# First attention: selected and local scores of two head groups as two 64-row tiles, job pairs on one output bank

## What is computed

```python
ks = partial_rope(rms_norm(k_s, ks_gain), cos_t, sin_t)
k_blocks = ks.reshape(B, n_sel, SEL_LEN, G, Dh)      # n_sel = 512 / 64 = 8, top = min(8, 8)
s = jnp.einsum('bqgrd,bgqnld->bgrqnl', qi, kg).astype(f32) * scale
s = jnp.where(mask, s, NEG)                          # keys at or before the query
p = softmax(s); o_s = einsum(p, vg)
# local branch: the same with kw, vw, over the last WINDOW = 256 positions and the query itself
# MLA: 8 heads, 96 query/key dimensions, 64 value dimensions, causal
```

## Time and profile before

| | us |
|---|---|
| median of 3 runs | 2212.72 |
| lowest, highest | 2210.98, 2212.72 |
| span of the profiled execution | 2210.5 |
| TensorE busy in it | 2158.2 (98%) |
| VectorE, ScalarE, GpSimd busy | 1498.9, 946.0, 1195.8 |
| first attention, first NSA score to first MLA score | 209.4 to 300.8 |

### The profile page before, as it was taken

The page is one execution under the profiler, slowest core; times in us unless marked ns, Lnnn a source line. Parts: engine busy times, 40 slices in busy tenths (PEclk is TensorE's granted clock), DMA queues, the critical chain, the costliest instruction groups (busy, mean ns, idle before and its releaser), DMA issues.

```text
span 2210.5 us, 33160 instructions
## 1 busy us (share of the span) xinstructions
PE 2158.2 (98%) x12377; PEld 1842.0 (83%) x12377; DVE 1498.9 (68%) x2234; ACT 946.0 (43%) x1891; POOL 1195.8 (54%) x594
## 2 busy tenths in 40 slices
PE   6999999999999999999999999999999999999997
PEld 4788888877899988887887898888897887889886
DVE  6834777554666592897646777677996727777676
ACT  3254663011556510544743555512545725455412
POOL 4747403776477677745016654577653037544675
PEclk9999999999999999999999999999999999999999
DMA  8322102522133233222002222322322002222221
GB/s 323 153 77 89 55 30 84 190 89 96 58 115 107 105 140 133 93 105 86 1 1 95 96 78 113 113 95 79 113 81 75 1 32 84 86 106 115 95 95 57
DMA packets 32776, 206.78 MB, mean 94 GB/s; under 512 B 4080, under 2 KB 4336, under 8 KB 11632
## 3 DMA queue, kind: packets, MB, share of 16 engines
q1 hardware_dynamic: 32192, 200.27, 24.8%
q10 hardware_dynamic: 432, 4.46, 0.5%
HBM read 202.61 MB, written 2.10 MB: 93 GB/s over the span
## 4 chain that ended last, share of the span: by engine, by line
PE 88%; DVE 6%; issue 1%; ACT 1%; DMA 1%; DVEq 1%; POOL 1%; POOLq 0%; SPq 0%; ACTq 0%
PE PS L1126 18%; PE PS L1128 18%; PE PS L1127 18%; PE PS L1605 5%; PE PS L1617 5%; PE PS L1382 3%; PE PS L1381 3%; PE PS L1383 3%; PE PS L1631 3%; PE PS L1457 2%; PE PS L1459 2%; PE PS L1458 2%; PE PS L1256 1%; PE PS L1259 1%; PE PS L1258 1%
## 5 line engine op out<-in xcount | busy, mean ns | idle before, releaser
L665 POOL TENSOR_TENSOR w_hi<-raw,zero_c 128x512 fp32r<-128x512 f32 (+1 forms) x135 | 281.6, 2104 | 545.5 <-PE PS L1128 544.3
L669 POOL TENSOR_TENSOR w_lo<-raw,w_hi 128x512 fp32r<-128x512 f32 (+1 forms) x135 | 365.0, 2723 | 5.8
L1126 PE MATMUL PS<-b_hi,w_hi 128*128 128x512 f32 x512 | 203.1, 397 | 0.9 <-POOL w_lo L888 0.9
L1127 PE MATMUL PS<-b_lo,w_hi 128*128 128x512 f32 x512 | 203.0, 396 | 0.0
L1128 PE MATMUL PS<-b_hi,w_lo 128*128 128x512 f32 x512 | 203.0, 396 | 0.0
L3345 DVE TENSOR_TENSOR b_lo<-a_all,b_hi 128x512 fp32r<-128x512 f32 x44 | 162.6, 3733 | 49.3 <-ACT b_hi L2490 49.3
L1126 PE MATMUL PS<-f_hi,w_hi 128*128 128x512 f32 x448 | 177.6, 397 | 0.7 <-DVE f_lo L2647 0.7
L1128 PE MATMUL PS<-f_hi,w_lo 128*128 128x512 f32 x448 | 177.6, 396 | 0.0
L1127 PE MATMUL PS<-f_lo,w_hi 128*128 128x512 f32 x448 | 177.6, 396 | 0.0
L688 POOL TENSOR_TENSOR w_lo<-raw,w_hi 128x512 fp32r<-128x512 f32 x48 | 70.9, 1477 | 92.9 <-ACT w_hi L2482 92.9
L1126 PEld LDWEIGHTS PS<-b_hi,w_hi 128*128 128x128 f32 x512 | 96.4, 188 | 24.6 <-POOL w_lo L888 1.1
(11 more groups left out here) (586 smaller groups left out, 6868.7 us busy)
## 6 DMA issues: line engine op xcount, KB each, us to landing
raw<-slabs_dram SPq DMA_DIRECT2D x161, 1024.0 KB, 4.8
aux<-ada_dram SPq DMA_DIRECT2D x18, 512.0 KB, 5.7
ada_first<-ada_dram SPq DMA_DIRECT2D x11, 512.0 KB, 14.1
cmpw<-cmpw_dram ACTq DMA_DIRECT2D x2, 2048.0 KB, 12.7
ada_late<-ada_dram SPq DMA_DIRECT2D x8, 512.0 KB, 3.2
ada_last<-ada_dram SPq DMA_DIRECT2D x8, 512.0 KB, 6.4
xT<-xT_dram SPq DMA_DIRECT2D x1, 2048.0 KB, 9.3
out_dram<-t SPq DMA_DIRECT2D x4, 512.0 KB, 3.2
```

Source lines behind the costliest of these rows:

```text
L665: high = nc.gpsimd.tensor_tensor(w_hi[:, slot, c], raw[:, slot, c], zero[:, 0:c.stop - c.start], ALU.add)
L669: low = nc.gpsimd.tensor_tensor(w_lo[:, slot, c], raw[:, slot, c], w_hi[:, slot, c].bitcast(f32), ALU.subtract)
L1126: nc.tensor.matmul(out, a_hi_, b_hi_, start=start, stop=False)
L1127: nc.tensor.matmul(out, a_hi_, b_lo_, start=False, stop=False)
```

## The change

The jobs of one head index r and one branch b come as twins: group 0's job directly ahead of group 1's, with equal masks and key ranges. Their query and key slices are cut to the 64 partitions of their group. `Plan` weaves a twin's tiles: (m, j=3), (m+1, j=3), (m, 0), (m+1, 0), (m, 2), (m+1, 2), (m, 1), (m+1, 1). TensorE issues both score calls in the first of the two steps and none in the second; values and transposes stay one tile a step. Ahead of them it waits for the mask of the tile two before the first one. The two outputs of a twin share a bank, 256 columns each, and twins alternate between the two output banks; VectorE finishes both jobs behind the last value tile of the second. MLA's jobs and the second block's are not twins.

```diff
-                    group = [m + 1, m] if m + 1 < len(jobs) and is_pair(jobs[m + 1]) else [m]
+                    group = [m, m + 1] if jobs[m]["twin"] else [m + 1, m] if m + 1 < len(jobs) and is_pair(jobs[m + 1]) else [m]
...
-                self.first, self.last = {vs[0] for vs in at_job}, {vs[-1] for vs in at_job}
+                self.first, self.last = {vs[0] for vs in at_job}, {vs[-1]: (m,) for m, vs in enumerate(at_job)}
+                self.out = [(6 + m % O_BANKS, 0) for m in range(len(jobs))]
+                self.freed = [m - O_BANKS + 1 for m in range(len(jobs))]
+                for m in range(0, len(jobs), 2):
+                    if jobs[m]["twin"]:
+                        for g in (0, 1):
+                            self.out[m + g] = (6 + m // 2 % O_BANKS, 256 * g)
+                            self.freed[m + g] = m - 2
+                        del self.last[at_job[m][-1]]
+                        self.last[at_job[m + 1][-1]] = (m, m + 1)
...
+                    woven = woven and not jobs[m]["twin"]
...
-            for g in range(GROUPS):
-                h = g * REP + r
-                for b, kslot, v in ((1, 0, lambda kb, g=g: z[:, 1, kb, 384 + 64 * g:448 + 64 * g]),
-                                    (2, 1, lambda kb, g=g: z_tail[:, kb, TAIL_VW + 64 * g:TAIL_VW + 64 + 64 * g])):
-                    nsa_jobs.append(job(qT_n[:, 2 * r + g, :], kT_n[:, kslot, :], v,
+            for b in (1, 2):
+                for g in range(GROUPS):
+                    h = g * REP + r
+                    v = ((lambda kb, g=g: z[:, 1, kb, 384 + 64 * g:448 + 64 * g]) if b == 1 else
+                         (lambda kb, g=g: z_tail[:, kb, TAIL_VW + 64 * g:TAIL_VW + 64 + 64 * g]))
+                    rs = slice(64 * g, 64 * g + 64)
+                    nsa_jobs.append(job(qT_n[rs, 2 * r + g, :], kT_n[rs, b - 1, :], v,
                                         O_nsa[:, :, 64 * h:64 * h + 64], strip2[:] if b == 2 else causal,
-                                        window=b == 2, coef=sigm(h, b), mode="add"))
+                                        window=b == 2, coef=sigm(h, b), mode="add", twin=1 + g))
...
-                    if step < n:
-                        m, c, j, _ = plan.scores[step]
+                    twin = step < n and jobs[plan.scores[step][0]]["twin"] == 1
+                    second = 0 < step < n and jobs[plan.scores[step - 1][0]]["twin"] == 1
+                    for at_step in () if step >= n or second else (step, step + 1) if twin else (step,):
+                        m, c, j, _ = plan.scores[at_step]
...
-                        if step >= s_banks:
-                            pe.wait_ge(scores_masked, g0 + step - s_banks + 1)
-                        nc.tensor.matmul(PS[:, step % s_banks, 0:128 * nb], query_tile(jobs[m]["q"][c], j),
+                        need = step + 1 if twin else at_step
+                        if need >= s_banks:
+                            pe.wait_ge(scores_masked, g0 + need - s_banks + 1)
+                        nc.tensor.matmul(PS[:, at_step % s_banks, 0:128 * nb], query_tile(jobs[m]["q"][c], j),
...
-                        if v in plan.first and m >= O_BANKS:
-                            pe.wait_ge(out_used, m0 + m - O_BANKS + 1)
+                        bank, o0 = plan.out[m]
+                        if v in plan.first and plan.freed[m] > 0:
+                            pe.wait_ge(out_used, m0 + plan.freed[m])
                         for b in range(nb):
-                            last = nc.tensor.matmul(PS[:, 6 + m % O_BANKS, 64 * j:64 * j + 64],
+                            last = nc.tensor.matmul(PS[:, bank, o0 + 64 * j:o0 + 64 * j + 64],
...
                         if v in plan.last:
-                            m = plan.values[v][0]
                             dve.wait_ge(pv_done, v0 + v + 1)
-                            finish(jobs[m], m, plan.sums[m][0] % 8)
+                            for m in plan.last[v]:
+                                finish(jobs[m], m, plan.sums[m][0] % 8, *plan.out[m])
```

More of the change, by code:

```diff
@@ L1011, in key_range, with job @@
             return lo, j - lo + 1
-        def job(q, k, v, out, strip=None, window=False, coef=None, mode="set", turned_by=None, vector=True):
-            return dict(vector=vector, q=q if isinstance(q, tuple) else (q,), k=k, v=v, out=out, strip=strip, window=window, coef=coef, mode=mode, turned_by=turned_by)
+        def job(q, k, v, out, strip=None, window=False, coef=None, mode="set", turned_by=None, vector=True, twin=0):
+            return dict(twin=twin, vector=vector, q=q if isinstance(q, tuple) else (q,), k=k, v=v, out=out, strip=strip, window=window, coef=coef, mode=mode, turned_by=turned_by)
         def sigm(h, b):
@@ L1594, in attend @@
                 for step in range(plan.steps):
-                    if step < n:
-                        m, c, j, _ = plan.scores[step]
+                    twin = step < n and jobs[plan.scores[step][0]]["twin"] == 1
+                    second = 0 < step < n and jobs[plan.scores[step - 1][0]]["twin"] == 1
+                    for at_step in () if step >= n or second else (step, step + 1) if twin else (step,):
+                        m, c, j, _ = plan.scores[at_step]
                         lo, nb = key_range(jobs[m], j)
                         if banks_ready:
-                            banks_ready(step)
-                        if jobs[m]["turned_by"] and step % TT == 0:
+                            banks_ready(at_step)
+                        if jobs[m]["turned_by"] and at_step % TT == 0:
                             pe.wait_ge(mla_act, jobs[m]["turned_by"])
                             pe.wait_ge(mla_dve, jobs[m]["turned_by"])
-                        if step >= s_banks:
-                            pe.wait_ge(scores_masked, g0 + step - s_banks + 1)
-                        nc.tensor.matmul(PS[:, step % s_banks, 0:128 * nb], query_tile(jobs[m]["q"][c], j),
+                        need = step + 1 if twin else at_step
+                        if need >= s_banks:
+                            pe.wait_ge(scores_masked, g0 + need - s_banks + 1)
+                        nc.tensor.matmul(PS[:, at_step % s_banks, 0:128 * nb], query_tile(jobs[m]["q"][c], j),
                                          jobs[m]["k"][:, 128 * lo:128 * (lo + nb)], start=True, stop=True
@@ L2879, in join, with finish @@
                                            ).then_inc(combined, 1)
-            def finish(jb, m, of):
+            def finish(jb, m, of, bank, o0):
                 inv = stats[:, 216 + 4 * (m % 2):220 + 4 * (m % 2)]
@@ L2886, in finish @@
                     then(V.tensor_tensor(inv, inv, jb["coef"], ALU.mult))
-                o = PS[:, 6 + m % O_BANKS, 0:TT * HD].rearrange("p (t d) -> p t d", t=TT)
+                o = PS[:, bank, o0:o0 + TT * HD].rearrange("p (t d) -> p t d", t=TT)
                 by = inv.unsqueeze(2).to_broadcast([P, TT, HD])
```

## The result

The changed kernel takes 2228.33 us in the median of 4 runs (2225.61 to 2230.98) against 2212.7 before: 1.0073 times as long, with a 95% interval of 1.006 to 1.0087. That is 15.6 us slower, where 5.0 were forecast, and the median lies 1.8 us above the upper end of the range. Executions that took far longer than the others of their kernel are left out of every median here: three of e2's six (2309 to 2311 us; in the profiled one TensorE had half the clock from 231 to 398 us) and single ones of e3, of e17 and of the kernel before. The profiled execution has a span of 2228.9 us (2210.5 before).

A forecast was written before the change was run, and what follows sets the result against it. TensorE's own slots were taken to bound the first attention, VectorE barely keeping up. Passages 12.8 less overlap 7.8, with 0 for the order, added 5.0 us to 2212.7: 2217.7 us, range 2208.5 to 2226.5.

The forecast's parts named there:

- Step 1: NSA scores: cutting operands from 128 to 64 rows by itself gains nothing, as matmul time goes by columns.
- Step 2: Both groups' score calls for a tile, issued together on separate rows and banks, partly overlap: 7.8 us saved, bounds 0 to 16.4.
- 3T: Pair's length, T being half a call: second call's first instruction (B1) waits for the first call's second (A2).
- rival (a): Score pairs overlap wholly, taking 2T, two half calls: -3.6 us, 2209.1 us; chance 0.14.
- Step 3: Entering and leaving the 64-row form around each of 32 pairs costs TensorE 0.40 us: 12.8 us, at least 7.7.
- Rival (b): Passages into and out of 64-row form cost only 0.24 us, with 3T: 2212.6 us; chance 0.12.
- Step 4: New job order, stricter mask wait and adjacent VectorE finishes: taken as 0, up to 3 us in the bound.
- Step 5: One output bank for a pair, and the first MLA job's wait for it: nothing, up to 0.3 us once.
- Rival (d): TensorE gaps bring one or two more half-clock stretches, +2 to +4 us, or avoid one, -1.7; no chance of its own.
- the 0.09 us: Sign: load idle of 0.09 us ahead of each pair's first score and the value matmul behind, 64 of each kind.
- The middle stretch longer by 2 to 3 us: Sign in the profile after: steps 30 to 63 of the first attention grow by this much, MLA unchanged.
- VectorE's rival: VectorE's bursts decide, at most 3 us; sign: TensorE waits for masks above 3 us in all; no chance of its own.

The follow-up runs named there:

- e2: Kernel before with only the NSA score queries and keys cut to 64 rows, old order, single calls: 2232.13 to 2233.06 us, ratio 1.0092.
- e3: Changed kernel with an output bank for each job and each job finished behind its own last tile: 2235.78 us, ratio 1.01.
- e17: Changed kernel without the root of the MLA norms and without three of the four multiply-adds of each NSA finish: 2211.50 us.
- e19: e2 without the root of the MLA norms and without three of the four multiply-adds of each NSA finish: 2232.95 us.
- e11: Changed kernel at 128 rows, each score in its own step, second finish three steps later; woven order and shared banks stay: 2220.8 us, ratio 1.0035.
- e1: Changed kernel with twins' queries and keys over 128 rows again; order, pairs, shared banks and double finishes stay: 2228.89 us, ratio 1.0075.
- e14: Changed kernel without the root of the MLA norms (no table loads), finishes whole: 2227.57 us; the kernel before without the root took 2208.94.
- e9: Changed kernel with the second job of each pair finished three steps behind the first: 2223.3 us, ratio 1.0056.
- e10: e9 with 128 rows in place of 64: 2222.9 us, ratio 1.0042.
- e18: e1 without the root of the MLA norms and without three of the four multiply-adds of each NSA finish: 2211.43 us.
- e20: Changed kernel without three of the four multiply-adds of each NSA finish, root and table loads kept: 2216.81 us, ratio 1.0018.
- e12: e9 with 64 rows only for the heads r > 1 (steps 32 to 63), 128 rows before: 2222.4 us, ratio 1.0046.
- e13: e9 with VectorE copying the j = 2 tile for the second twin and ScalarE the j = 3 tile: 2232.97 us, ratio 1.0098.
- e21: e9 without the root of the MLA norms, so without the two table loads, all multiply-adds kept: 2217.07 us, ratio 1.0027.

## Why the prediction was wrong

The sum was 12.8 - 7.8 + 0 = +5.0. Two of its three terms were about the columns and passages of TensorE, and those now give -3.6. The third, taken at nothing, is 19.2 by difference (15.6 + 3.6), with the clock's share in it, and it carries the result.

**Step 1, 64 rows alone gain nothing:** right. In e19 each call is slower by the passage alone.

**Step 2, the pair's overlap:** that the two calls overlap was right, that B1 waits for A2 was not. I took 3T because of that wait; measured is 2T, rival (a)'s: 0.84 in the chain for a 384-key pair is 0.64 + 0.20, where 3T would be 0.97 + 0.20. The saving is 16.4 and not 7.8. Of the two rules of the Trainium skill, TensorE: Matmul & The Clock Gate, Part 3 (The mechanism), this trace agrees with the span model, which gives 2T: the first instructions of the two calls start 7 ns apart and the second ones 6. It disagrees with an order of starts A1, A2, B1, B2. That the four stand so in the instruction stream was my assumption, and the trace doesn't show it. With the value matmuls' 0.20 a 384-key pair is 0.26 us cheaper than before (1.30 - 0.84 - 0.20), not the 0.08 dearer that I had.

**Step 3, the passages:** right to a hundredth of a us: 0.40 forecast, 0.39 to 0.40 in e19, and 0.20 ahead of each pair and 0.20 behind it in the changed kernel (e2's 0.31 compares a kernel with a short low stretch, the one before, and has no profile). Rival (b) is out. The rule of the Trainium skill that I weighed there, TensorEngine Tiling (Array Packing), Key Properties, holds in these traces, each side with 0.20 us.

**Step 4, the order, the stricter wait and the double finish:** this is the step that failed. I took 0 and bounded it by 3 us; the woven order with the shared banks measured 8.4 (e11), and with the pair's common wait and the double finish 16.1 (e1), at 128 rows and so without steps 2 and 3. There are four faults in it. I weighed mean against mean over an 8-step cycle (3.1 us of VectorE against 3.2 of TensorE), and a balance of means says nothing of the queue inside the cycle: from the first finish to the start of TensorE's pair it took 3.53 us (265.45 to 268.98), of which TensorE waited 1.06. In the steps up to 30 it is worse: in e14 the two finishes alone take 4.3 us (228.48 to 232.73). I called the pair's own passages its cover, but the 0.40 stood in TensorE's 3.2 already, and value matmuls stood there at the price of score calls (0.86 and 0.65, not 0.81 and 0.61); put right, my own balance has VectorE late by nothing to 0.4 us a cycle, with no cover left to pay for it. At 2T the pair is also shorter than I had it: the faster TensorE became, the less it had to hide VectorE. And I priced the order's effect only through the masks; e11 has neither common wait nor double finish, and its transposes wait 6.5 us for ScalarE's copies, a queue that stands nowhere in my sum. I had written that VectorE was busy 39.95 of 46.90 us; that row called for a range, not a zero.

That VectorE's queue is the cause of most of it is shown by e14 to e17: without the root the change costs 18.6 us, and with three of four multiply-adds gone as well 3.4. TensorE's -3.6 does not appear in the medians: after against e1 is -0.6 us, e9 against e10 +0.4, e17 against e18 +0.1. A queue that holds TensorE back explains the first two; for the third, with VectorE light, it is not shown. At full clock, from step 30 to 75, the row tiles do give 0.7 (69.8 against 70.5), 0.6 (66.3 against 66.9) and 0.8 us (63.7 against 64.5).

**Step 5, the shared bank:** taken at nothing, and no run measures it alone; e3 shows that without it 7.5 us more are lost.

**Rival (d), the clock:** the mechanism was on the list, at +2 to +4 us and for one or two stretches of 3.5 us. There was one stretch, of 31 us; by the table it takes 13.7 us more than before, more than the 12.4 by which steps 0 to 29 grew. This is bookkeeping and not a cause by itself: e1 loses 7.1 to the clock and its first stretch is only 3.0 us shorter, since at 128 rows the waits show instead. What is shown is that in the profiles of this stage each fall, e2's aside, stands in or shortly behind a gap of TensorE of 0.9 to 2.9 us, and that the gaps come from both ScalarE's table loads (worth 5.1 us of clock loss: 15.5 less 10.4) and VectorE's finishes (10.6: 15.5 less 4.9). A gap alone does not foretell a fall: 1.18 us in e17 and 2.04 in e18 brought none.

**The signs to look for:** the 0.09 us were there. The last transpose ahead of the pair shown starts at 274.40 and streams for 0.11, and the pair's load starts at 274.60; the pair's second instructions start at 275.03 and stream for 0.32, and the next load starts at 275.44. There are 32 such places ahead of pairs and 32 behind them, not 64 of each kind. "The middle stretch longer by 2 to 3 us" was 5.8 over steps 30 to 75, and the sign that I set for VectorE's rival, waits for masks above 3 us in all, came: 4.0 behind step 30 alone. The chances followed the sum: slower had 0.53, so the direction was the likeliest, but the range missed by 1.8 us because step 4's bound of 3 us was worked out from the same balance that was wrong.

Open: why the half-clock stretch lasts 31 us in one piece after, but some 10 us in e20 and some 14 in pieces in e1 (7.1 lost). It is not fixed by the kernel: of the changed kernel's own four executions two took 2226 us at a mean clock of 0.992 and two 2231 at 0.990 and 0.989. The row tiles may lengthen it (e9 loses 7.0, e10 3.6), but e12 and e13 give no clean answer, and e2, which varied the rows alone, has no profile that counts.

## What to carry to other kernels

With a second engine at 85% of the bounding one, an order that sets two large tiles behind each other cost 8.4 us here, more than twice the 3.6 of matmul slots to be saved. Lay the two queues against each other step by step, not as means, and ask what hides the helper once the leader is faster. A row-tiled pair of float32 scores between 128-row work pays 0.40 us for its passages and saves one whole call, so by these numbers it breaks even at 256 keys (0.43) and gains above, if the engines behind it can follow. A new gap in TensorE is to be priced with the half-clock stretch that may follow it (here 31 us behind gaps of 1.2), not with its own length alone.

## What the hardware showed that I had not expected

Two float32 calls on separate row tiles run wholly side by side, though each is two instructions: their first ones start 7 ns apart, their second ones 6, and it is 0.64 us for a 384-key pair once the passage is taken off. Their four weight loads pass in 0.30 us.

The half clock can hold for long after a short gap while TensorE's rows show it busy: from 229 to 260 us, with 4.86 to 5.00 us busy in each 5 us, after gaps of 1.19 and 1.26 us; in e21 some 17 us from within one of 1.64.

VectorE's work came back almost whole in the time, though TensorE is busy 91% of that stretch: finishes lighter by 6.7 us behind step 30 (53.74 to 47.05) shortened it by 6.1 us (69.8 to 63.7, in e17 and e20 alike).

A small VectorE instruction was slow while GpSimd worked. The multiplication of 4 columns in a finish takes 0.17 us in the mean behind 256 us; ahead of it, with GpSimd's multiplications beside it, it takes 0.49 in the kernel before, 0.39 in the changed one and 0.64 in e14, and 1.17 in the gap of e14 shown above. No run changed GpSimd's work, so that this is the reason is not shown.
